# A two-layer decoder with experts: turned rows in the experts' order, gather rows split from the residual, router by slices

## The chip, the cores and the metric

The kernel runs on one core of a Trainium2 chip. The metric is the device time of one execution in microseconds (us), median of the runs. The core has PE (matrix engine, TensorE), DVE (vector), ACT (scalar), POOL and SP, each with its own instruction stream; they meet at semaphores. SP issues nearly all loads from HBM; sixteen DMA engines carry them. SBUF and PSUM (eight banks of 128 x 512 f32) are on chip.

## The reference

Batch 1, 256 tokens, width 1024, all f32, two layers. Cut to what matters here:

```python
h = rms_norm(x, norm2_g[l]) * (1.0 + sc2) + sh2        # sc2, sh2, g2: 1024 each, from c @ ada_w[l] + ada_b[l]
x = x + g2 * moe_ffn(h, ...)

scores = sigmoid(h @ w_router)                         # 64 experts in 8 groups
sel = scores + router_bias
gscore = sum of the two highest sel of each group; the 4 best groups are kept
idx = top 6 of sel among the kept groups
w = scores[idx] / sum(scores[idx]) * 2.5
routed = sum over chosen e of w_e * swiglu(h, w_gate_up[e], w_down[e])     # 1024 -> 2*256 -> 1024
shared = swiglu(h, shared_gate_up, shared_down)
```

Ahead of it stands an attention with norm and residual of its own in each layer (a dilated one in layer 0, a latent one in layer 1).

## The kernel before, in words

**Passes.** The experts of a layer are sorted by their count of tokens. `plan_passes` lays 64 experts in 22 passes of 128 slots (2 to 5 experts each). For each pass p PE gathers the tokens of its slots, with one-hot matrices `sel` that DVE makes out of `slot_of` or `slot_at` (`gather_half`, line 881: for two passes together, 256 slots, one half of the eight row groups at a time; 16 matmuls of `h_hi` and `h_lo` by `sel` per half). ACT copies the result into `xg` (`gathered`, 1335). `gate_up` (902) multiplies by the expert's weights in two halves, each of which frees its weight units; then silu, `hidden`, `middle` (transposes), `down` (944), and `scatter` (919) adds the rows back to tokens in banks 0 to 3, one pass late. The expert weights are stored with row p*8+k on partition p, so a gathered row group k holds rows p*8+k.

**Loads.** A unit is 1 MB of SBUF, 17 of them. The first experts (ranks 0 to 4) are fixed, as experts 0 to 4 are always placed first, and are loaded ahead (`EARLY_UNITS`, `LATE_UNITS`, `LAST_UNITS`). The others are chosen by count. SP waits for `order` (line 664), which says which expert has which rank, then issues each load as soon as its unit has been read by its user before (`wait_read`). The first, for pass 2, need half 0 and half 1 of passes 0 and 1 to be read; later ones need down projections.

**From the norm to pass 0.** `norm` on ACT (1282) and DVE (1529): sum of squares, square root, reciprocal, then two diagonal matrices `diag_r` with the tokens' scales. PE's `ada_sums` and `ada_columns` (729) turn a row of modulation (`row_of[g]`, copied from bank 7 by ACT in `ada_rows`, 1274) into columns with four matmuls; `norm_transposes` (713) multiplies x by `diag_r`, which turns and scales it at once: 16 matmuls of 128 contiguous columns of x into banks 0 to 3. DVE (banks 0, 2) and ACT (banks 1, 3) apply `amp` and `mod` and write hT, whose row group k holds rows k*128+p. In `experts` (845) PE computes the router's logits (16 matmuls, after all of hT), turns hT back into token rows (16 transposes), and a first half of the shared expert. ACT takes the sigmoid and copies the turned-back rows into `h_hi` as fp32r; `interleaved` (382) makes that write the rows in the order p*8+k. DVE does the routing (1604 on): biases, group maxima, a mask of groups by multiplying and adding, top six, `chosen`. It then computes `h_lo` = h - `h_hi`. PE forms ranks and counts; DVE makes `slot_of`, `sel`, `keys`, `hot`, `flag`; PE gathers pass 0 and 1, transposes the tables, and computes `order`, `places`, `at_ps`; `gate_up(0)` waits for `order`, then come `gate_up(1)` and the tables of overflow slots, which this input does not use.

An f32 matmul stands as two records in the trace, an fp32r one as one. Most matmuls pass through the helper on line 708, transposes through 711, ACT copies through 1234, SP loads of experts through 580 and of ring chunks through 548, so those lines stand for many places; the tile names tell them apart.

**In the attention of layer 0** SP's loads pass in one order: ring chunks of `kv_ada_w`, `w_router` (637), two rows of `router_bias` (640), two small ones, then ten chunks of `ada_w`, each as its ring place comes free. PE's `ada_columns(g)` for g=1, 2, 6, 4 stands between projections and heads.

## Time and profile before

| | |
|---|---|
| median of 3 runs | 1367.34 us (1365.87 to 1367.44) |
| the profiled execution | 1366.1 us, span of its instructions 1364.2 us, mean granted PE clock 0.933 |
| busy share | PE 82%, DVE 31%, ACT 19%, POOL 0% |
| moved from HBM | 500 MB, 367 GB/s over the span |

```profile
## 2 busy tenths in 40 slices
PE   6999887997798687777768889899779778777775
...
PEclk9998998999798899889889999899989979988979
DMA  9999996799999999999976715679999999999995
```

Each digit is a tenth of the busy share in one of 40 slices of 34 us. Slices 1 to 6 are the attention of layer 0, 7 to 20 its experts, 20 to 25 the attention of layer 1, the rest its experts. The DMA row is at 9 through the experts and lower about the beginning of each expert stage and in the attention of layer 1.

### The profile page before, as it was taken

The numbers are of one execution on the slowest core, as the hardware profiler recorded it, in microseconds if no ns is written. First come the engines' busy times: TensorE is split into PE (matmuls) and PEld (weight loads), VectorE is DVE, ScalarE is ACT, GpSimd is POOL, SyncE is SP. The second block draws the span as 40 slices with busy tenths as digits, with TensorE's granted clock in tenths as the row PEclk, the third lists the DMA queues.
The fourth block names the chain that finished last, engine by engine and source line by source line (L and its number), as shares of the span: only waits on it lengthen the run. The fifth ranks groups of instructions, "written<-read, shape, count | busy, mean of one in ns | idle before, by whom it ended". The sixth has DMA issues, their size and how long they took to land.

```text
span 1364.2 us, 17322 instructions
## 1 busy us (share of the span) xinstructions
PE 1114.0 (82%) x6720; PEld 619.4 (45%) x6720; DVE 422.6 (31%) x1026; ACT 253.1 (19%) x572; POOL 0.4 (0%) x5
## 2 busy tenths in 40 slices
PE   6999887997798687777768889899779778777775
PEld 4886466544243243233327467754424324322332
DVE  1397546321121121112132576532112112111213
ACT  1122513111011110101022263311101111010100
POOL 0000000000000000000000000000000000000000
PEclk9998998999798899889889999899989979988979
DMA  9999996799999999999976715679999999999995
GB/s 349 396 407 407 355 401 258 294 382 424 422 424 424 423 424 423 425 423 422 423 294 262 250 36 185 247 284 390 424 423 423 425 422 424 423 425 423 423 423 214
DMA packets 99914, 502.26 MB, mean 368 GB/s; under 512 B 11865, under 2 KB 37366, under 8 KB 44534
## 3 DMA queue, kind: packets, MB, share of 16 engines
q1 hardware_dynamic: 99366, 500.92, 90.1%
q8 instruction: 55, 0.90, 0.3%
q10 hardware_dynamic: 464, 0.20, 0.1%
q14 instruction: 29, 0.24, 0.0%
HBM read 500.04 MB, written 1.05 MB: 367 GB/s over the span
## 4 chain that ended last, share of the span: by engine, by line
SPq 42%; PE 33%; DMA 13%; DVE 6%; issue 4%; ACT 2%; DVEq 0%; ACTq 0%
SPq L580 39%; PE bank L708 27%; DMA w_gu<-in_moe_w_gate_up 4%; DMA w_gu_x<-in_moe_w_gate_up 4%; DMA ring<-in_ada_w 3%; SPq L666 3%; PE bank L1091 2%; DMA ring<-in_moe_w_gate_up 2%; PE bank L711 2%; PE bank L926 1%; DMA ring<-in_a_w_o 1%; DVE acc L1511 1%; PE bank L1072 1%; ACT p_sb L1311 1%; SPq L640 1%
## 5 line engine op out<-in xcount | busy, mean ns | idle before, releaser
L708 PE MATMUL bank<-w_gu,ring 128*32 128x512 f32 (+1 forms) x1088 | 341.5, 694 | 81.4 <-DMA w_gu<-in_moe_w_gate_up 55.5
L708 PEld LDWEIGHTS bank<-w_gu,ring 128*32 128x32 f32 (+1 forms) x1088 | 89.9, 134 | 213.1 <-issue 213.1
L708 PE MATMUL bank<-ring 128*32 128x512 f32 (+1 forms) x384 | 162.1, 689 | 21.6 <-DMA w_gu<-in_moe_w_gate_up 21.6
L708 PE MATMUL bank<-w_gu_x,ring 128*32 128x512 f32 (+1 forms) x320 | 144.6, 669 | 25.8 <-DMA w_gu<-in_moe_w_gate_up 21.2
L1729 DVE TENSOR_TENSOR hh<-sg,bank 128x256 f32<-128x256 f32 x44 | 27.4, 624 | 426.4 <-ACT sg L1344 426.4
L708 PE MATMUL bank<-w_gu,hhT 128*32 128x512 f32 (+1 forms) x576 | 147.2, 599 | 2.3 <-DMA w_gu<-in_moe_w_down 2.3
L708 PE MATMUL bank<-w_dn,ring 128*32 128x512 f32 x240 | 101.0, 788 | 24.0 <-DMA w_gu<-in_moe_w_gate_up 9.8
L1746 DVE SCALAR_TENSOR_TENSOR y_lo<-bank,w_slot,y_hi 128x512 fp32r<-128x512 f32 x88 | 62.0, 746 | 177.1 <-ACT y_hi L1234 177.1
L1344 ACT ACTIVATE sg<-bank 128x256 f32<-128x256 f32 x44 | 16.9, 384 | 504.7 <-PE bank L708 504.7
L708 PE MATMUL bank<-sel,h_hi 128*128 128x256 f32 x352 | 87.8, 289 | 0.0
L708 PE MATMUL bank<-sel,h_lo 128*128 128x256 f32 x352 | 84.2, 279 | 0.0
L1234 ACT ACTIVATE y_hi<-bank,w_slot 128x512 fp32r<-128x512 f32 x88 | 55.6, 683 | 149.4 <-PE bank L708 149.4
L926 PE MATMUL bank<-y_hi,st 128*128 128x512 f32 x176 | 73.7, 419 | 9.8 <-DVE y_lo L1746 9.8
L1234 ACT ACTIVATE ring<-bank 128x512 f32<-128x512 f32 x88 | 47.8, 595 | 156.1 <-PE bank L708 156.1
L1511 DVE SCALAR_TENSOR_TENSOR acc<-ring,csilu,acc 128x2048 f32<-128x2048 f32 x28 | 65.7, 2347 | 15.6 <-DMA ring<-in_ada_w 15.3
L926 PE MATMUL bank<-y_lo,st 128*128 128x512 f32 x176 | 69.2, 393 | 0.0
L708 PEld LDWEIGHTS bank<-w_gu_x,ring 128*32 128x32 f32 (+1 forms) x320 | 34.1, 130 | 75.1 <-issue 75.0
L708 PEld LDWEIGHTS bank<-sel,h_lo 128*128 128x128 f32 x352 | 66.5, 189 | 0.0
L708 PEld LDWEIGHTS bank<-sel,h_hi 128*128 128x128 f32 x352 | 66.0, 188 | 0.3
L708 PE MATMUL bank<-hT,ring 128*128 128x256 f32 (+2 forms) x192 | 61.3, 473 | 5.1 <-DMA w_gu<-in_moe_w_gate_up 5.1
L708 PEld LDWEIGHTS bank<-ring 128*32 128x32 f32 (+1 forms) x384 | 38.9, 133 | 58.2 <-issue 58.2
L708 PE MATMUL bank<-ring,hhT 128*32 128x512 f32 (+1 forms) x160 | 58.1, 596 | 0.6 <-DVE hhT L1736 0.6
(285 smaller groups left out, 1575.3 us busy)
## 6 DMA issues: line engine op xcount, KB each, us to landing
w_gu<-in_moe_w_gate_up SPq DMA_DIRECT2D x126, 1024.0 KB, 25.9
w_gu<-in_moe_w_down SPq DMA_DIRECT2D x68, 1024.0 KB, 26.3
ring<-in_ada_w SPq DMA_DIRECT2D x44, 1024.0 KB, 11.3
ring<-in_moe_w_gate_up SPq DMA_DIRECT2D x44, 1024.0 KB, 26.8
w_gu_x<-in_moe_w_gate_up SPq DMA_DIRECT2D x38, 1024.0 KB, 25.3
w_dn<-in_moe_w_gate_up SPq DMA_DIRECT2D x30, 1024.0 KB, 25.8
ring<-in_moe_w_down SPq DMA_DIRECT2D x16, 1024.0 KB, 26.1
w_dn<-in_moe_w_down SPq DMA_DIRECT2D x14, 1024.0 KB, 26.8
```

The source lines that it names most:

```text
L580: sp.dma_start(dst, src).then_inc(sem(f"unit_in{u}"), 16)
L640: sp.dma_start(bias_row[:, n, :], t["moe_router_bias"][n:n + 1, :].broadcast_to([P, E]))\
L666: index = {j: sp.value_load(tab_i[0:1, j:j + 1], min_val=0, max_val=E - 1) for j in sorted({j for _, j, _ in items if j != "shared"})}
L708: return nc.tensor.matmul(o, a, b, start=first, stop=last)
L711: return nc.tensor.transpose(o, a, const("ident")[0:rows, 0:rows])
L926: last = nc.tensor.matmul(bank[2 * ti + half][:, :], st[:, ti * P:(ti + 1) * P], y[:, half * 512:(half + 1) * 512], start=first and y is y_hi,
L1091: last = nc.tensor.matmul(bank[c][:, ti * N:(ti + 1) * N], hT[:, 2 * j + k, ti * P:(ti + 1) * P], qkv_rows[j][:, k, c * N:(c + 1) * N], st ...
L1234: return nc.scalar.activation(o, i, ACT.Copy, **kw)
L1344: nc.scalar.activation(sg[:, :], bank[b][:, 0:FE], ACT.Silu).then_inc(sem(f"silu_done{l}"), 1)
L1511: ins = v.scalar_tensor_tensor(out=acc[:, :], in0=w, scalar=csilu[:, k:k + 1], in1=acc[:, :], op0=ALU.mult, op1=ALU.add)
L1729: v.tensor_tensor(hh[:, :].rearrange("s (f p) -> s p f", f=FE // P), sg[:, :].rearrange("s (p f) -> s p f", f=FE // P), bank[b][:, FE:2 * ...
L1746: last = v.scalar_tensor_tensor(out=y_lo[:, c], in0=bank[6 + half][:, :], scalar=w_slot[:, :], in1=y_hi[:, c].bitcast(F32), op0=ALU.mult, ...
```

## The change

**Row order.** `norm_transposes` takes every eighth column of x (`every_8th`) in norms 1 and 3, so hT's group k holds rows p*8+k. `w_router`, the shared gate and up weights, the shift, the scale and the norm gain are brought into that order: by other access patterns of the loads, by `ada_columns`, which for those rows takes every eighth element of a strip with 16 matmuls of 64 weights instead of four of 128, and by a small tile `rows_pk`, filled by three loads on ACT's queue near the start.
**Gather rows.** `h_hi` and `h_lo` are split from the raw x times the token's scale, in norm (ACT copies x to `h_hi`, DVE subtracts), both written contiguously. The gathers read every eighth column of them. The shift and scale are applied afterwards, when ACT moves the gathered rows (`gathered`: four Identity operations with bias and scale instead of two copies). The 16 transposes back and the four strided copies and subtractions fall away.
**Order of work.** The router's matmuls follow slice by slice behind hT. A dummy sigmoid brings ACT's table load into norm. `row_of` is copied by DVE. The shared half is split in pieces around ranks, gather and places. `order` and `places` come before the tables; `gate_up(0)` no longer waits for `order`; the table transposes and `at_ps` go between the halves of passes 0 and 1; in layer 1 the gate's two matmuls go from the norm to between passes 0 and 1. DVE's group mask is one operation instead of five.

```diff
-            h_hi = sb("h_hi", [P, NT, KT, P], F32R, scope=moe)
+            h_hi = sb("h_hi", [P, NT, D], F32R, scope=moe)
+        def every_8th(tokens, k):
+            return tokens[:, k:k + D - KT + 1:KT]
...
-                                 t["moe_w_router"].rearrange("l (k p) e -> p (l k) e", p=P)).then_inc(sem("router_in"), 16)
+                                 t["moe_w_router"].rearrange("l (p k) e -> p l (k e)", p=P)).then_inc(sem("router_in"), 16)
...
+                            tokens = x[:, ti, k * P:(k + 1) * P] if n == 2 else every_8th(x[:, ti, :], k)
-                if n == 3:
-                    gate_half(3, 0)
-                    gate_half(3, 1, 6)
...
+                strips = {3: 4, 6: 4, 4: 2}.get(g, 0)
+                for m in range(4 if strips else 0):
+                    last = mm(bank[7][:, m:4 * strips:4], row_of[g][:, m * P:(m + 1) * P], const("quarters")[:, 0:strips], True, True)
+                if strips < 4:
+                    q0, at = (2, 2 * strips + 4 * (strips > 0)) if g in (1, 4) else (0, 0)
+                    for u in range(2):
+                        for k in range(KT):
+                            last = mm(bank[7][64 * u:64 * u + 64, at + k:at + k + 1], every_8th_of_strip(row_of[g], k),
+                                      const("quarters")[:, q0 + u:q0 + u + 1], True, True)
...
-                for j in range(4):
-                    ti, half = j // 2, j % 2
-                    for k in range(4):
-                        last = tr(bank[j][:, k * P:(k + 1) * P], hT[:, 4 * half + k, ti * P:(ti + 1) * P])
-                    last.then_inc(sem("h_ps"), 1)
-                                last = mm(o, h[:, ti, 4 * half + kk, :], sel[:, ti, :], ti == 0 and h is h_hi,
+                                last = mm(o, every_8th(h[:, ti, :], 4 * half + kk), sel[:, ti, :], ti == 0 and h is h_hi,
-                    if p == 0:
-                        pe.wait_ge(sem("order"), l + 1)
+                gate_up(0)
...
+                if l == 1:
+                    for half, b in enumerate((3, 7)):
+                        mm(bank[b][:, :], const("quarters")[:, 2 + half:3 + half].broadcast_to([P, P]), row_of[5][:, :], True, True)\
+                            .then_inc(sem("gate_ps"), 1)
+                gate_up(1, (0,))
...
-                gate_up(0)
-                gate_up(1)
+                gate_up(1, (1,))
...
+            for n in range(2):
+                act.dma_start(rows_pk[:, n, 0:2, :], t["ada_b"][n:n + 1, 3 * D:5 * D].rearrange("a (s p k) -> p (a s) k", p=P, k=KT))\
+                   .then_inc(sem("mask_in"), 16)
+            act.dma_start(rows_pk[:, :, 2, :], t["norm2_g"].rearrange("l (p k) -> p l k", k=KT)).then_inc(sem("mask_in"), 16)
-                    ada_rows(ADA_IN_WO[n // 2])
+                    nc.scalar.activation(small[:, 34:35], eps_c, ACT.Sigmoid)
+                    act.wait_ge(sem("xn_ready"), 2 * n + 2)
+                    copy(h_hi[:, 0, :], x[:, 0, :], scale=small[:, 4:5]).then_inc(sem("h_act"), 1)
-                        last = copy(xg[l][i % 2][:, k:k + 2, :].rearrange("p k c -> p (k c)"), bank[banks[b]][:, :])
+                        last = nc.scalar.activation(xg[l][i % 2][:, k, :], bank[banks[kk // 2]][:, (kk % 2) * N:(kk % 2 + 1) * N],
+                                                    ACT.Identity, bias=mod[:, 24 + 48 * l + k:25 + 48 * l + k], scale=amp[:, 1 + 2 * l, k:k + 1])
...
+                        last = v.scalar_tensor_tensor(out=h_lo[:, ti, :], in0=x[:, ti, :], scalar=small[:, 4 + ti:5 + ti],
+                                                      in1=h_hi[:, ti, :].bitcast(F32), op0=ALU.mult, op1=ALU.subtract)
-                link(V, v.tensor_tensor(gmask[:, :, :], gleft[:, :, 0:G], gsc[:, :, 0:G], ALU.not_equal))
...
+                link(V, v.tensor_tensor(gmask[:, :, :], gleft[:, :, 0:G], gsc[:, :, 0:G], ALU.is_equal))
+                link(V, v.scalar_tensor_tensor(out=ch, in0=gmask[:, :, :].unsqueeze(3).broadcast_to([P, NT, G, 8]), scalar=-big, in1=ch,
+                                               op0=ALU.mult, op1=ALU.add))
-                for j in range(4):
-                    dve.wait_ge(sem("h_act"), 4 * l + j + 1)
-                    v.tensor_tensor(interleaved(h_lo, j), in_order(bank[j]), interleaved(h_hi, j).bitcast(F32), ALU.subtract)\
-                        .then_inc(sem("h_dve"), 1)
```

## Rows read from the trace of the kernel before

**Rows 1.** page, part 3: the DMA queue of ACT's loads: packets, MB, share of 16 engines
```profile
q10 hardware_dynamic: 464, 0.20, 0.1%
```

**Rows 2.** windows: length, busy PE, PEld, DVE, ACT, POOL; PE clock, DMA share, GB/s
```profile
144.00:152.00 8.00, 6.33 (x66) 3.23 (x64) 6.36 (x29) 6.24 (x23) 0.00 (x0) 1.00 0.54 136
...
230.00:252.00 22.00, 20.30 (x128) 14.63 (x128) 15.92 (x68) 6.35 (x9) 0.00 (x0) 1.00 0.22 72
270.00:280.00 10.00, 9.87 (x64) 5.54 (x68) 2.17 (x5) 2.36 (x4) 0.00 (x0) 1.00 0.74 291
...
863.00:869.00 6.00, 5.70 (x26) 5.70 (x27) 1.82 (x6) 0.36 (x2) 0.00 (x0) 0.50 0.97 388
1000.00:1300.00 300.00, 234.04 (x1408) 102.05 (x1408) 53.49 (x112) 36.80 (x67) 0.00 (x0) 0.91 1.01 424
```

**Rows 3.** timeline of the SP queue in the attention of layer 0 (start, length)
```profile
139.24 7.64 SPq L640 DMA_DIRECT2D bias_row<-in_moe_router_bias  x2
...
147.87 19.45 SPq L548 DMA_DIRECT2D ring<-in_ada_w  x10
```

**Rows 4.** timeline of the SP queue, layer 0, first loads of the chosen experts
```profile
249.93 1.43 SPq L580 DMA_DIRECT2D w_gu_x<-in_moe_w_gate_up  x2
...
278.30 0.33 SPq L580 DMA_DIRECT2D xn<-in_moe_w_gate_up  x1
```

**Rows 5.** timeline, layer 0, from the norm to the first pass (start us, length us)
```profile
216.07 1.87 PE L708 MATMUL bank<-cst,kT 128*128 128x4 f32 x8 [2.26 <-ACT kT L1234]
...
217.80 5.37 PE L708 MATMUL bank<-xn,x 128*128 128x128 f32 x32
...
224.33 3.75 PE L708 MATMUL bank<-w_router,hT 128*128 128x64 f32 x32 [1.16 <-issue]
...
232.35 0.48 DVE L1628 TENSOR_TENSOR choice<-choice,gleft 128x64 f32<-128x64 f32 x2
...
234.51 3.85 DVE L1638 TENSOR_TENSOR h_lo<-bank,h_hi 128x512 fp32r<-128x512 f32 x4
...
235.69 0.31 PEld L708 LDWEIGHTS bank<-cst,chosen 128*64 128x64 f32 x4
...
239.69 0.28 PE L708 MATMUL bank<-sel,h_lo 128*128 128x256 f32 x1
...
243.23 0.28 PE L708 MATMUL bank<-sel,h_lo 128*128 128x256 f32 x1
...
245.04 1.10 PE L708 MATMUL bank<-hot,rtT 64*128 64x64 f32 x8 [0.35 <-DVE rtT L1709]
...
246.07 3.65 PE L708 MATMUL bank<-w_gu_x,ring 128*64 128x512 f32 x16
```

**Rows 6.** timeline, layer 1, the same place
```profile
863.30 1.87 PE L708 MATMUL bank<-cst,kT 128*128 128x4 f32 x8 [2.56 <-ACT kT L1234]
...
870.86 1.88 PE L708 MATMUL bank<-kT,cst 128*128 128x512 f32 x4
```

**Rows 7.** groups by line and form: weight loads, DVE (| busy us, mean ns)
```profile
L708 PEld LDWEIGHTS bank<-sel,h_lo 128*128 128x128 f32 x352 | 66.5, 189 | 0.0
...
L1638 DVE TENSOR_TENSOR h_lo<-bank,h_hi 128x512 fp32r<-128x512 f32 x8 | 7.7, 1030 | 0.0
...
L1600 DVE TENSOR_TENSOR x<-x,junk 128x512 f32<-128x512 f32 x8 | 5.5, 692 | 0.3
...
L1614 DVE TENSOR_TENSOR gsc<-gsort 128x16 f32<-128x16 f32 x2 | 0.4, 187 | 0.1
...
L1621 DVE TENSOR_TENSOR gmask<-gleft,gsc 128x16 f32<-128x16 f32 x2 | 0.3, 174 | 0.1
```

**Rows 8.** timeline behind pass 0 (ACT, PE), and a group of ACT by form
```profile
263.90 1.09 ACT L1234 ACTIVATE ring<-bank 128x512 f32<-128x512 f32 x2 [3.38 <-PE bank L708]
...
264.01 3.65 PE L708 MATMUL bank<-w_dn,hhT 128*64 128x512 f32 x16
...
L1292 ACT ACTIVATE hT<-bank,mod,amp 128x256 f32<-128x256 f32 x12 | 6.1, 559 | 17.8 <-PE bank L708 17.8
```

More of the change, by code:

```diff
@@ L845, in experts, with shared_part @@
             def experts(l):
+                n = 2 * l + 1
                 pe.wait_ge(sem("router_in"), 16 * 5)
[L848 to L860 removed]
+                for j, (ready, turn) in enumerate((("hT_dve", 2 * n + 3), ("hT_act", 2 * n - 1), ("hT_dve", 2 * n + 4),
+                                                   ("hT_act", 2 * n))):
+                    pe.wait_ge(sem(ready), turn)
+                    for k in (2 * j, 2 * j + 1):
+                        for ti in range(NT):
+                            last = nc.tensor.matmul(bank[4][:, ti * E:(ti + 1) * E], hT[:, k, ti * P:(ti + 1) * P],
+                                                    w_router[:, l, k, :], start=k == 0 and ti == 0, stop=k == KT - 1,
+                                                    skip_group_check=True)
+                last.then_inc(sem("logits"), 1)
+                def shared_part(j, f, b, k0, k1):
                     w = use(("sgu", l, j))
[L862 removed]
+                    for k in range(k0, k1):
                         last = mm(bank[b][:, f * N:(f + 1) * N], w[:, k, f * P:(f + 1) * P], hT[:, k, :], k == 0, k == KT - 1)
[L864 removed]
+                    if f == FE // P - 1 and k1 == KT:
                         used(("sgu", l, j), last)
[L867 to L868 removed]
+                pe.wait_ge(sem("gate_sb"), 4 * l + 2)
+                shared_part(0, 0, 6, 0, KT)
+                shared_part(0, 1, 6, 0, 4)
                 pe.wait_ge(sem("chosen"), l + 1)
@@ L898, in gather_pair, with gate_up @@
                             for h in (h_hi, h_lo):
-                                last = mm(o, h[:, ti, k, :], sel[:, ti, 0:P], ti == 0 and h is h_hi, ti == NT - 1 and h is h_lo)
+                                last = mm(o, every_8th(h[:, ti, :], k), sel[:, ti, 0:P], ti == 0 and h is h_hi, ti == NT - 1 and h is h_lo)
                     last.then_inc(sem(f"gath_done{l}"), 1)
-                def gate_up(p):
+                def gate_up(p, halves=(0, 1)):
                     pe.wait_ge(sem(f"xg_ready{l}"), 2 * (p // 2) + 2)
-                    if p == 0:
-                        pe.wait_ge(sem("order"), l + 1)
-                    elif p >= 2:
+                    if p >= 2:
                         pe.wait_ge(sem(f"st_ready{l}"), p)
-                    for half in range(2):
+                    for half in halves:
                         for j in positions(p):
@@ L1294, in norm @@
                     last.then_inc(sem("hT_act"), 1)
+                    if n != 2 and j == 1:
+                        copy(h_hi[:, 1, :], x[:, 1, :], scale=small[:, 5:6]).then_inc(sem("h_act"), 1)
             def attention(l):
@@ L1330, in experts @@
                     .then_inc(sem("score"), 1)
-                for j in range(4):
-                    act.wait_ge(sem("h_ps"), 4 * l + j + 1)
-                    copy(interleaved(h_hi, j), in_order(bank[j])).then_inc(sem("h_act"), 1)
                 def gathered(i, half, banks=(4, 7)):
                     act.wait_ge(sem(f"gath_done{l}"), 2 * i + half + 1)
-                    for b in (1, 0):
-                        k = 4 * half + 2 * b
-                        last = copy(xg[l][i % 2][:, k:k + 2, :].rearrange("p k c -> p (k c)"), bank[banks[b]][:, :])
+                    for kk in range(4):
+                        k = 4 * half + kk
+                        last = nc.scalar.activation(xg[l][i % 2][:, k, :], bank[banks[kk // 2]][:, (kk % 2) * N:(kk % 2 + 1) * N],
+                                                    ACT.Identity, bias=mod[:, 24 + 48 * l + k:25 + 48 * l + k], scale=amp[:, 1 + 2 * l, k:k + 1])
                     last.then_inc(sem(f"xg_ready{l}"), 1)
@@ L1371, in experts @@
                         act.wait_ge(sem(f"gath_done{l}"), p + 1)
-                        for b, k in ((7, 4), (4, 0)):
-                            last = copy(xg[l][0][:, k:k + 4, 0:P], bank[b][:, :].rearrange("p (k c) -> p k c", c=P))
+                        for k in range(KT):
+                            last = nc.scalar.activation(xg[l][0][:, k, 0:P], bank[4 if k < 4 else 7][:, (k % 4) * P:(k % 4 + 1) * P],
+                                                        ACT.Identity, bias=mod[:, 24 + 48 * l + k:25 + 48 * l + k],
+                                                        scale=amp[:, 1 + 2 * l, k:k + 1])
                         last.then_inc(sem(f"xg_ready{l}"), 1)
@@ L1529, in norm @@
             def norm(n, outs):
+                if n != 2:
+                    g = ADA_IN_WO[n // 2]
+                    dve.wait_ge(sem("ada_sums"), SUMS_TURN[g])
+                    v.tensor_copy(row_of[g][:, :], bank[7][:, :]).then_inc(sem("row_sb"), 1)
                 norm_scale(n)
```

108 lines of the change are left out of this document (53 added, 55 removed).

## The prediction

> **What bounds the kernel now.** I read the windows first, then the SP timeline, then PE, ACT and DVE between the norm and the first expert pass. In the passes the DMA engines are full: 424 GB/s at a share of 1.01 over 300 us, while PE is busy 234 of them [rows 2]. There a faster or slower engine is worth nothing as long as the load queue stays full. The time can only move where that queue runs dry. It does so at three kinds of place. (1) In the attention of layer 0 it moves 136 GB/s for 8 us [rows 2], behind SP's load of the router and its bias [rows 3]. (2) Before the first pass of each layer all prefetched units are full; the queue stands at 72 GB/s from 230 to 252 us [rows 2] until half 0 of pass 0 has been read, and the first chosen expert is requested at 249.93 [rows 4]. (3) It is dry once more, 0.74 in 270 to 280 [rows 2], until pass 1's down projection is over and units come free at 278.30 [rows 4]. From there it is full to the end of the layer. So the gain of a layer is not how much earlier pass 0 begins, but how much earlier pass 1 ends, since ten loads of 1 MB are through by then in both cases.
>
> **The path before pass 0, layer 0, step by step.** All of it is PE, ACT and DVE in series [rows 5].
> Row copy: `row_sb` moves from ACT, where it stood behind the square root, to DVE right behind `ada_sums`. The 128x512 copy costs about 0.69 like other DVE work of that size [rows 7]; DVE is idle there. PE's columns begin at 214.85 instead of 216.07: 1.2 off. Layer 0's columns (g=3) keep their 8 records.
> Router: it now follows each slice of hT instead of all of it. Its last quarter of 3.75 us [rows 5] is 0.95. The transposes (5.4 us, [rows 5]) end near 222.0; ACT turns the last slice until 223.3, though its copy to h_hi and a table load are now ahead of it (the load falls into its idle time, and the copy ends at 222.3). Logits at 224.35 instead of 228.1: 3.7 off, the 1.2 included.
> Routing chain on DVE: two multiplies, two adds, one scale and two memsets give way to one operation. The adds alone took 0.48 [rows 5], the multiplies as much; the saving is 1.15. Chosen at about 229.8 for 234.6: 4.8 off.
> Split: h_lo's 3.85 us stood between `chosen` and `slot_of` [rows 5]; it goes into DVE's waits in the norm, where two operations of 1024 columns at about 1.2 us fit beside the transposes. The 16 turns of hT on PE go as well. PE now needs 1.4 us for the ranks, DVE about 1.1 for slots and selection: the gather starts at 232.3 instead of 239.5, 7.2 off.
> After the gather: 2.8 us lay before pass 0. Now there are the order and places (0.9), a quarter of the shared half (0.9), and the wait for ACT, whose evacuation is four Identity operations of 0.56 (about 1.95 in a row) instead of two copies in 1.09 [rows 8]: 2.2. **Pass 0 starts 7.8 us earlier**, near 238.25 [rows 5]. The order is ready at 236.5, well before SP can use it.
> What is moved behind it: the table transposes (0.65) and `at_ps` (1.10, [rows 5]) now stand between the halves of passes 0 and 1. They were ahead of pass 0, so they count against the 7.8 at the place that matters, the end of pass 1: +1.7. DVE's copies of the tables and its selection for the next pass end some 2 us before PE is through with the second half of pass 1; half the cover would be left if each took 1 us more.
> ACT's longer evacuation, once per pass: it starts at 263.90 and would end at 265.85; the down projection (264.01, 3.65 long, [rows 8]) needs the bank for its second half at 265.85. That is a tie, 0.1 per pass, 0.2 in all.
> Layer 0: 7.8 - 1.7 - 0.2 = **5.9 us off**.
>
> **Layer 1.** The same, with two differences. Its columns (g=5) are now 32 narrow records instead of 8 in 1.87 us [rows 6]. Four weight loads of 64 columns took 0.31 at full clock [rows 5], some 0.06 apart; at the half clock granted here [rows 2] twice that, so 3.7 for 1.87, which costs 1.85 and eats the early start. The two gate matmuls (four records, 1.88, [rows 6]) leave the norm, where PE would otherwise have waited for hT for most of that time, so 0.4 is gained, and they come back between passes 0 and 1 for 1.75. 5.9 - 1.85 + 0.4 - 1.75 = **2.7 off**.
>
> **Ahead of that.** The router's weights are read in rows of 2 KB instead of 256 bytes: 256 pieces for 2048. SP's bias load behind it took 7.64 us for two small loads [rows 3]; the next ada chunks went out only at 147.87. The DMA engines lost 8 x (1 - 136/424) = 5.4 us. From there to the first pass the chain is DMA, so that is returned almost whole, unless the hold is backlog of other loads. Bounds 0 and 5.4. Against it stand the columns of g=1, 2 and 4: 72 more narrow records, 4 us of PE in the attention, 2 of them before SP's router load; I take **4.5 off**.
> The three new ACT loads fetch 768 pieces of 32 bytes. The ACT queue's 464 packets took 0.1% of 16 x 1364 us, 47 ns each [rows 1], so 48 pieces per engine cost up to 2.3 us beside the first weight block, for which PE waits. Bounds 0 and 2.3; I take **+1.5**, nearer to the upper end since that block is what the start waits for.
>
> **The term that nothing in the trace shows: strided weight loads.** hT's transposes, every gather and the narrow columns now load PE's weights with a step of 32 bytes. Before, all were contiguous. A load of 128 columns takes 189 ns [rows 7] and gathers follow each other in 117 ns, from 239.69 to 243.23 for 31 [rows 5], so the weight load (107 of it for the columns) is what sets the gather's pace as much as the 256 columns do. A lower bound is 0. The upper bound comes from DVE: with a strided output 512 columns took 1030 ns, without 692 [rows 7], 0.66 ns more per element, up to about 1.7 ns each; reading every 8th element cost 187 for 174 with 16 elements, 0.8 ns each [rows 7]. At 1.7 ns the 128 columns take 107 ns longer. Transposes: 24 full-clock records, +2.6. First gather: 32, +3.4. Both gathers before the end of pass 1: +3.4. That is 9.4 per layer, 1.7 more for layer 1's columns, and 1.5 in the attention: 22 us. I take 0 as the likelier end, because PE has its own read path, of which these DVE rows show nothing, and PE's moving operand shows it fetching twice as fast as its weights are; but the opposing rows are the nearest there are, and the price is as large as the gain.
> The Trainium skill speaks against the change here: SBUF — State Buffer, section "Door 1: The DMA port swizzle", says that SBUF is fetched in lines of 16 bytes and that accesses which leave the line every time pay. A step of 32 bytes does. DVE's rows agree with it; no row here shows it for PE. By that rule the time is that of the first rival; without it, that of the sum.
>
> **Sum.** -5.9 - 2.7 - 4.5 + 1.5 = -11.6, on the profiled execution's 1366.1: 1354.5. The median of the runs stands 1.2 above it, so 1355.8.
>
> **Rivals.**
> *Strided weight loads at half pace* (slower). 1355.8 + 22 = 1377. It decides from a price of about 55 ns per load on, where the gain is gone. For it: DVE's two rows. Against: in the passes PE has 66 of 300 us free [rows 2], so the other 18 gathers of each layer cost nothing. 31%.
> *The early pass is given back*: pass 0 moves, pass 1 does not, since the tables between the halves make DVE's selection late, or the SP hold is backlog and stays. Without the router's 4.5 and half of the layers' 8.6 the time is 1364.5. For it: the hold begins while earlier loads are still landing. 15%.
> *The clock stays up*: before the columns in both layers PE is idle 2.3 to 2.6 us and then runs at 0.50 (863 to 869, [rows 2]). The idle time becomes 1.1 to 1.3. If it does not fall, up to 3 us a layer come back: 1351. It is a part of the likeliest case's range.
> *The change does not do what it says*, as more passes or other experts: the routing is the same arithmetic; 1%.
>
> **How the numbers follow.** Forecast 53%: 1350 to 1361. Given back 15%, 1361 to 1369. Strided 31%, 1369 to 1378. To leave out no more than two in ten the range must reach into the strided case: 1349 to 1378. A measurement of this kernel can tell about 0.2%, 2.7 us, from no change. Faster: 53, two thirds of 15, and a light price of the stride: 64%. Same: 9%. Slower: 27%.
>
> **What would show it.** Gathers 117 ns apart, or 220. Weight loads of h_lo 189 ns, or near 300. Pass 0 at 238 less what was gained ahead. SP's two bias loads in 1 to 2 us, not 7.6. In 144 to 152 us above 400 GB/s. The interval from the last attention matmul to the first chosen load shorter by 7 to 8 us, and that to the end of pass 1 by 6. I am wrong if the gathers keep their pace and the time still does not fall, or if the window before pass 0 shortens and the end of the layer stays.

## The result, and the profile after

| | kernel before | changed kernel |
|---|---|---|
| median | 1367.07 us (4 runs) | 1396.36 us (4 runs, 1387.44 to 1397.49) |
| ratio | | 1.0212, 95% interval 1.0166 to 1.0257 |
| profiled execution | 1366.1 us | 1387.4 us, span 1385.6, mean granted PE clock 0.947 |
| PE busy | 82% | 86% |

The change costs 29 us (a fifth execution, not in the median, took 1401.33) where I had forecast a gain of 12. The profiled execution of the changed kernel is its fastest one; it is 21 above that of before. So 8 of the 29 us aren't in the trace.

The groups by line and form say first what is different (busy us, mean ns of one):

```profile
L709 PEld LDWEIGHTS bank<-sel,h_lo 128*128 128x128 f32 x352 | 118.9, 338 | 0.0
...
L1353 ACT ACTIVATE ring<-bank,mod,amp 128x256 f32<-128x256 f32 x176 | 84.9, 563 | 256.5 <-PE bank L709 256.5
...
L1577 DVE SCALAR_TENSOR_TENSOR h_lo<-x,small,h_hi 128x1024 fp32r<-128x1024 f32 x4 | 5.1, 1275 | 0.0
...
L709 PEld LDWEIGHTS bank<-cst,kT 128*64 128x64 f32 x32 | 3.5, 216 | 2.1 <-DVE kT L1559 2.1
```

A weight load of 128 columns of `h_lo` takes 338 ns for 189 [rows 7], one of 64 narrow columns 216. The operations that I had sized from other rows came out as sized: ACT's evacuation 563 ns (559 in [rows 8]), DVE's h_lo 1275 for my 1.2 us. The timeline of layer 0, PE unless marked, shows what that does to the pace. It answers to [rows 5]:

```profile
95.10 3.55 PE L709 MATMUL bank<-cst,ada_row 128*64 128x1 f32 x32
...
191.76 4.43 PE L709 MATMUL bank<-cst,ada_row 128*128 128x2 f32 x40
...
218.72 1.04 PE L709 MATMUL bank<-acc,cst 128*1 128x512 f32 x8
220.98 1.05 PE L709 MATMUL bank<-cst,kT 128*128 128x4 f32 x8 [1.21 <-DVE kT L1559]
222.55 7.91 PE L709 MATMUL bank<-xn,x 128*128 128x128 f32 x32 [0.52 <-DVE xn L1550]
230.29 3.68 PE L860 MATMUL bank<-w_router,hT 128*128 128x64 f32 x32
...
239.43 1.26 PE L709 MATMUL bank<-chosen,cst 128*128 128x64 f32 x10 [0.21 <-DVE chosen L1668]
...
241.90 0.41 PE L709 MATMUL bank<-sel,h_lo 128*128 128x256 f32 x1
...
249.13 0.40 PE L709 MATMUL bank<-sel,h_lo 128*128 128x256 f32 x1
...
251.55 3.65 PE L709 MATMUL bank<-w_gu_x,ring 128*64 128x512 f32 x16 [0.21 <-ACT ring L1353]
```

Thirty gathers lie between 241.90 and 249.13: 241 ns apart, for 118 in [rows 5]. The transposes take 7.91 us for 5.37. Pass 0 begins at 251.55, 5.5 us later than before; I had said 7.8 earlier, and more with what was to be gained ahead. `ada_sums`, where my path begins, is at 218.72 for 212.76: 6.0 us are lost ahead of it already. The SP queue shows the two other places (start, length), which answer to [rows 3] and [rows 4]:

```profile
143.97 1.21 SPq L641 DMA_DIRECT2D bias_row<-in_moe_router_bias  x2
...
146.25 22.56 SPq L549 DMA_DIRECT2D ring<-in_ada_w  x10
...
255.41 0.89 SPq L581 DMA_DIRECT2D w_gu_x<-in_moe_w_gate_up  x2
...
289.79 0.33 SPq L581 DMA_DIRECT2D xn<-in_moe_w_gate_up  x1
```

The end of pass 1, my measure of a layer, moves from 278.30 to 289.79. And the windows (columns as in [rows 2]):

```profile
144.00:152.00 8.00, 8.00 (x84) 3.93 (x82) 6.38 (x29) 5.75 (x22) 0.00 (x0) 1.00 0.80 313
230.00:252.00 22.00, 21.58 (x124) 19.45 (x126) 10.83 (x69) 5.64 (x12) 0.00 (x0) 1.00 0.32 135
...
280.00:290.00 10.00, 10.00 (x48) 6.41 (x50) 1.18 (x3) 2.21 (x5) 0.00 (x0) 1.00 0.39 162
1000.00:1300.00 300.00, 252.76 (x1404) 124.41 (x1396) 53.91 (x114) 49.16 (x97) 0.00 (x0) 0.94 1.01 421
```

In 230 to 252 the queue moves 135 GB/s for 72, since the last prefetched units are asked for later than before; the dry place ahead of pass 1's end is now 280 to 290, at a share of 0.39. The last row holds a thing I had not looked for. In the passes PE has 47 of 300 us free, so it isn't the bound, the DMA share is 1.01 as before, and still 421 GB/s are moved and not 424. Over some 850 us of passes that is 6 us.

### The profile page after: what moved, and what is told of

Read it like the earlier page. It is cut to its first block, busy times and chain, and to the rows that moved or that the text cites. A ratio compares the mean times of both kernels' runs of the same rounds, so it can differ in the third digit from the quotient of the medians.

```text
span 1385.6 us, 17545 instructions
## 1 busy us (share of the span) xinstructions
PE 1186.8 (86%) x6792; PEld 702.0 (51%) x6792; DVE 419.7 (30%) x1017; ACT 286.1 (21%) x656; POOL 0.4 (0%) x5
## 3 DMA queue, kind: packets, MB, share of 16 engines
HBM read 500.07 MB, written 1.05 MB: 362 GB/s over the span
## 4 chain that ended last, share of the span: by engine, by line
PE 42%; SPq 36%; DMA 13%; DVE 4%; issue 4%; ACT 2%; DVEq 0%; ACTq 0%
PE bank L709 34%; SPq L581 33%; DMA w_gu<-in_moe_w_gate_up 4%; DMA w_gu_x<-in_moe_w_gate_up 4%; SPq L667 2%; PE bank L1101 2%; DMA ring<-in_moe_w_gate_up 2%; PE bank L930 2%; DMA ring<-in_ada_w 2%; PE bank L712 2%; PE bank L967 1%; DMA ring<-in_a_w_o 1%; ACT p_sb L1329 1%; PE bank L1082 1%; PE bank L860 1%
## 5 line engine op out<-in xcount | busy, mean ns | idle before, releaser
L709 PE MATMUL bank<-w_gu,ring 128*32 128x512 f32 (+1 forms) x1088 | 315.5, 651 | 73.3 <-DMA w_gu<-in_moe_w_gate_up 51.4
L709 PE MATMUL bank<-w_gu,hhT 128*32 128x512 f32 (+1 forms) x576 | 154.5, 607 | 0.0
L709 PE MATMUL bank<-sel,h_hi 128*128 128x256 f32 x352 | 146.3, 416 | 0.0
L709 PE MATMUL bank<-sel,h_lo 128*128 128x256 f32 x352 | 141.7, 403 | 0.0
L1353 ACT ACTIVATE ring<-bank,mod,amp 128x256 f32<-128x256 f32 x176 | 84.9, 563 | 256.5 <-PE bank L709 256.5
L709 PE MATMUL bank<-w_gu_x,ring 128*32 128x512 f32 (+1 forms) x320 | 126.5, 607 | 8.8 <-DMA w_gu<-in_moe_w_gate_up 5.7
L709 PEld LDWEIGHTS bank<-sel,h_lo 128*128 128x128 f32 x352 | 118.9, 338 | 0.0
L709 PEld LDWEIGHTS bank<-sel,h_hi 128*128 128x128 f32 x352 | 118.2, 336 | 0.1
L709 PE MATMUL bank<-w_dn,ring 128*32 128x512 f32 x240 | 83.1, 678 | 12.7 <-DMA w_gu_x<-in_moe_w_gate_up 9.2
L1771 DVE TENSOR_REDUCE w_slot<-bank 128x1 f32<-128x256 f32 x44 | 18.7, 424 | 145.2 <-PE bank L712 145.2
## 6 DMA issues: line engine op xcount, KB each, us to landing
w_gu<-in_moe_w_down SPq DMA_DIRECT2D x68, 1024.0 KB, 26.5
```

The costliest lines, as they stand in the source:

```text
L709: return nc.tensor.matmul(o, a, b, start=first, stop=last)
L1353: last = nc.scalar.activation(xg[l][i % 2][:, k, :], bank[banks[kk // 2]][:, (kk % 2) * N:(kk % 2 + 1) * N], ACT.Identity, bias=mod[:, 24 ...
L1771: v.tensor_reduce(w_slot[:, :], bank[5][:, 0:N], AX_X, ALU.add)
```

## The experiments

All of them are timed beside the kernel before on the same chip (its medians there: 1367.0 to 1368.3). Places are given as in the prediction: ada_sums, pass 0, end of pass 1.

### The strided weight loads

**a_gather, a_all, b_stride, deint.** The stride taken out of the changed kernel's gathers, then of all its weight loads, put into the gathers of the kernel before, and (deint) moved from PE to ACT and DVE.

```diff
 # a_gather (a_all does the same for norm_transposes and ada_columns)
-last = mm(o, every_8th(h[:, ti, :], 4 * half + kk), sel[:, ti, :], ...
+last = mm(o, h[:, ti, (4 * half + kk) * P:(4 * half + kk + 1) * P], sel[:, ti, :], ...
 # b_stride: the kernel before
-last = mm(o, h[:, ti, 4 * half + kk, :], sel[:, ti, :], ...
+last = mm(o, every_8th(h[:, ti, :, :], 4 * half + kk), sel[:, ti, :], ...
 # deint: h_hi, h_lo are [P, NT, KT, P]; by_k(row) = row.rearrange("t (q k) -> t k q", k=KT)
-copy(h_hi[:, 0, :], x[:, 0, :], scale=small[:, 4:5])
+copy(h_hi[:, 0, :, :], by_k(x[:, 0, :]), scale=small[:, 4:5])
```

> The changed kernel with one thing undone: the gathers load 128 contiguous columns of h_hi and h_lo, not every 8th (the experts then get other columns of the residual, so what they compute is changed). Theory 1, the strided weight load is what was lost: gathers 117 ns apart again instead of 242, the first gather 3.9 us shorter, the two before the end of pass 1 4.0 shorter, the same in layer 1: 15.8 us off the changed kernel, 1371.6 against its profiled 1387.4 and 1380 against its median of 1396. Theory 2, the loss is the narrow columns, the clock and the moved order: gathers get faster, the time stays above 1385.

> The changed kernel with all three strided weight loads made contiguous: gathers, transposes of the norms, and the narrow column matmuls (the values in them are then other ones). Theory 1: 15.8 us off for the gathers, 2.6 per layer for the transposes, and 96 narrow loads at 137 instead of 216 ns, 7.6 in all of which some 6 lie on a path that PE sets: 27 off, 1360 profiled and 1369 by the median. If the stride were all that my forecast missed, it would come to 1356. Theory 2: no lower than 1375.

> The kernel before with the gathers alone reading every 8th column of h_hi and h_lo (other columns than the experts want, so what they compute is changed). Theory 1: gathers 242 ns apart, 3.9 us in the first gather of each layer and 4.0 in the two before the end of pass 1: 1367 + 15.8 = 1383. Theory 2: gathers are longer but the passes hide all but the first, 1371 to 1375.

> The changed kernel, but ACT and DVE read the raw residual with the stride while they write h_hi and h_lo in expert order, so that the gathers load contiguous columns; what is computed stays the same. Theory 1: as much off as without the stride in the gathers, 15.8 us, if the copies of 1.13 (ACT) and 1.27 us (DVE) grow by no more than a factor of 2, since PE's transposes take 7.9 us beside them: 1371.6 profiled, 1380 by the median. Rival: the strided read on ACT or DVE takes so long that the last slices of hT come late, and each us of it comes back twice, once per layer: 1385.

| | median us | ratio to before | ada_sums L0 | pass 0 L0 | end of pass 1 L0 |
|---|---|---|---|---|---|
| before | 1368.3 | | 212.76 | 246.07 | 278.30 |
| changed | 1396.4 | 1.0212 | 218.72 | 251.55 | 289.79 |
| a_gather | 1419.4 | 1.0380 | 219.72 | 248.67 | 286.24 |
| a_all | 1373.6 | 1.0034 | 218.36 | 244.87 | 280.74 |
| b_stride | 1421.5 | 1.0391 | 214.48 | 251.29 | 289.03 |
| deint | 1387.6 | 1.0151 | 219.18 | 248.14 | 285.70 |

The times of a_gather and b_stride say nothing on the stride. Other values come out of layer 0, layer 1 then chooses other experts, and one more pass is run: 368 gathers of each kind for 352, 508.6 MB moved for 502.3. I hadn't thought of that when I chose an edit that changes the data. Their layer 0 up to the end of pass 1, which comes ahead of it, can be read: from ada_sums to pass 0 it takes 28.95 us without the stride in the gathers and 32.83 with it (3.9 less), and b_stride 36.81 for the 33.31 of before.

a_all computes other values too, but has the same number of passes and moves the same 502.3 MB as the changed kernel. It is 23 us faster; I had expected 27. deint, which computes the same, gains 9 where 16 were expected. Its gathers are back at 189 ns a load, and these are the copies that now carry the stride:

```profile
L1247 ACT ACTIVATE h_hi<-x,small 128x1024 fp32r<-128x1024 f32 x4 | 8.6, 2140 | 0.0
L1580 DVE SCALAR_TENSOR_TENSOR h_lo<-x,small,h_hi 128x1024 fp32r<-128x1024 f32 x4 | 8.3, 2078 | 0.6 <-ACT h_hi L1247 0.6
```

The strided read takes ACT 2140 ns for 1138 and DVE 2078 for 1275, but it stays beside PE's transposes: the first gather of layer 0 follows ada_sums after 22.85 us, as in the changed kernel (22.86). So it isn't this rival that eats the 7 us. Up to pass 0 deint gains what was expected, 3.9 us in each layer. From pass 0 to the end of pass 1 it gains 0.7 in layer 0 (37.56 for 38.24) and 2.0 in layer 1 (39.29 for 41.32), where 4.0 were expected. There the granted clock falls where that of the changed kernel's trace stays up. In two windows of deint, then in the same two of the changed kernel:

```profile
262.00:266.00 4.00, 4.00 (x12) 1.10 (x10) 1.43 (x8) 0.00 (x0) 0.00 (x0) 0.57 1.01 426
274.00:280.00 6.00, 4.17 (x15) 3.41 (x16) 1.70 (x3) 0.74 (x2) 0.00 (x0) 0.72 0.99 389
```

```profile
262.00:266.00 4.00, 4.00 (x30) 2.73 (x28) 2.08 (x8) 0.00 (x0) 0.00 (x0) 1.00 1.01 426
274.00:280.00 6.00, 3.54 (x16) 1.12 (x13) 1.50 (x3) 2.31 (x5) 0.00 (x0) 1.00 0.82 294
```

One such fall costs 1.7 us, by the block of b_order below. Two in layer 0 and one more than the changed kernel's in layer 1 (0.72 in 920 to 926, for 1.00) are 5.1, so 15.8 become 10.7; in the traces it is 10.5. Why they fall in one kernel and not in the other isn't shown.

**b_nat** puts a price on the strided gathers alone, on unchanged data: it writes the rows in plain order and reads them with the step.

```diff
 # the kernel before, h_hi and h_lo [P, NT, D]
 def interleaved(h, j):
-    return h[:, j // 2, :, :].rearrange("t k (c q) -> t c q k", c=KT)[:, 4 * (j % 2):4 * (j % 2) + 4, :, :]
+    return h[:, j // 2, 512 * (j % 2):512 * (j % 2) + 512]
 # gathers: h[:, ti, k, :]  ->  h[:, ti, k:k + D - KT + 1:KT]
```

> The kernel before with h_hi and h_lo written in natural order (a contiguous write for ACT and DVE instead of one with a step) and the gathers reading every 8th column; it computes the same. The stride theory: gathers 242 ns apart, first gather 3.9 us longer, the two before the end of pass 1 4.0 longer together, DVE's h_lo 1.4 shorter: 6.5 per layer, 1380. If the passes hid the later gathers: 1372.

1388.6 us, ratio 1.0166 (1.0144 to 1.0189): 20.8 us for the gathers of both layers, more than the 12.5 expected. The weight load and the gathers' pace are those of the changed kernel, and the writes of h_lo got shorter (ACT's of h_hi too, 602 ns for 1088):

```profile
L711 PEld LDWEIGHTS bank<-sel,h_lo 128*128 128x128 f32 x352 | 119.2, 339 | 0.0
...
L1641 DVE TENSOR_TENSOR h_lo<-bank,h_hi 128x512 fp32r<-128x512 f32 x8 | 5.0, 681 | 0.0
```

The first gather is 3.9 longer, as expected. From pass 0 to the end of pass 1 it takes 37.8 us for 32.2 in layer 0 and 37.7 for 32.2 in layer 1, 5.5 where two gathers of 16 loads at 123 ns make 4.0. The rest is about one fall of the clock, which in layer 0 stands at 0.66 in 275 to 280. DVE's 1.4 gave nothing: from `chosen` to the first gather it is 4.74 for 4.84. From the end of pass 1 to that of the passes of layer 0 (the next layer's first load of `b_w_dq`) it takes 426.5 us for 426.0: the other gathers are indeed hidden behind the DMA, as the prediction had it.

### The alignment of the weight buffers

In the compiled kernel before, `ring` begins at byte 33920 of a partition, 128 past a multiple of 256, and so do `w_gu_x`, `w_gu_0`, `w_dn`, `xn` and `hT`: 13 of the 17 units lie in these. `w_gu_1`, 4 units, begins at 195840, a multiple of 256. The change adds `rows_pk`, 192 bytes, ahead of it; it lies at 195520 then, 192 past. (The changed kernel also takes 512 bytes of DMA scratch for 1024, which my list of the change doesn't name, so all its tiles begin 512 bytes lower. That moves no distance to a multiple of 256; it was not tried alone.)

```diff
 # b_shift: the kernel before
 amp = sb("amp", [P, 5, KT])
+pad = sb("pad", [P, 48])
 # b_align: 32 instead of 48, and pad_x = sb("pad_x", [P, 32]) ahead of x
 # a_pad: the changed kernel
 rows_pk = sb("rows_pk", [P, 2, 3, KT])
+pad = sb("pad", [P, 16])
```

> The kernel before with one unused tile of 192 bytes per partition put where the changed kernel has rows_pk. It computes the same. In the passes the changed kernel moves 421 GB/s, and so do its variants with contiguous gathers, while the kernel before moves 424; with gathers made strided it still moved 424. Theory A: the 192 bytes shift the buffers w_gu_1 (4 of the 17 units) off the boundary on which they lay, and each 8 KB piece written there takes longer: 421 GB/s here too, 3 us per layer, 1373. Theory B: the rate is lost to ACT's longer evacuation or another engine's traffic: 424 GB/s, 1367 to 1368.

> The kernel before with two unused tiles of 128 bytes per partition, so that ring, w_gu_x, w_gu_0 and w_dn (128 bytes past a multiple of 256 before) and w_gu_1 (on a multiple before) all begin at a multiple of 256 bytes. Theory A, if what counts is the distance to a multiple of 256: the other 13 units get faster too, 426 to 430 GB/s in the passes and 1352 to 1362. If only 64-byte steps below 128 count, or under theory B: 424 GB/s and 1367.

> The changed kernel with 64 unused bytes per partition behind rows_pk, so that w_gu_1 lies on a multiple of 256 bytes again, as before the change. It computes the same. Alignment theory: 424 GB/s in the passes instead of 421 and 5.7 us off, 1390 by the median. Rival, the rate of the changed kernel is lost to ACT's longer evacuation as well: less than 2 us off.

| | w_gu_1 past 256 | the 13 others | GB/s, 1000 to 1300 | median us | ratio |
|---|---|---|---|---|---|
| before | 0 | 128 | 424 | 1367.8 (a_pad's: 1367.0) | |
| b_shift | 192 | 128 | 421 | 1373.5 | 1.0050 (1.0032 to 1.0068) |
| b_align | 0 | 0 | 427 | 1358.5 | 0.9938 (0.9917 to 0.9959) |
| a_pad | 0 | 128 | 423 | 1390.3 | 1.0171 (1.0152 to 1.0190) |

Windows of 1000 to 1300, b_shift, then b_align:

```profile
1000.00:1300.00 300.00, 239.07 (x1409) 104.56 (x1407) 54.65 (x115) 37.90 (x69) 0.00 (x0) 0.89 1.01 421
```

```profile
1000.00:1300.00 300.00, 235.94 (x1444) 106.06 (x1448) 53.44 (x113) 37.02 (x68) 0.00 (x0) 0.92 1.01 427
```

An unused tile alone makes the kernel before 5.7 us slower, and aligned buffers make it 9 faster. 64 unused bytes make the changed one 6.0 faster by the medians. That fits, but its interval and the changed kernel's (1.0166 to 1.0257) overlap, so by itself it would not show it. That the rate is lost to ACT's evacuation falls: a_pad has it and runs at 423.

### What is left without stride and shift

**a_all_pad** is a_all with the 64 bytes; it too computes other values in the same number of passes.

> The changed kernel with contiguous weight loads in gathers, transposes and columns (the values in them are then other ones) and with w_gu_1 on a multiple of 256 bytes again. If only the stride and the alignment were missing in my forecast, it gives 1356. If the narrow columns (4.8 by the added ones), the tables moved between the halves and terms I over-valued before the gather also count, 1367 to 1369, the same as before.

1359.1 us, ratio 0.9950 (0.9932 to 0.9968). The stride in all three places is the 31.2 us between a_pad and this. The forecast was 1355.8, so it is 3 us off once both are out. The expectation that other terms would bring it back to 1367 was wrong. But the parts of the sum do not hold, as the next runs show.

**b_cols** adds narrow columns to the kernel before, on unchanged data, with the step of the change.

```diff
 # ada_columns of the kernel before
+for m in range({1: 12, 2: 12, 4: 16, 5: 12}.get(g, 0)):
+    u, k = m % 2, m // 2
+    last = mm(bank[7][64 * u:64 * u + 64, 16 + k:17 + k], row_of[g][:, k:k + 512 - KT + 1:KT],
+              const("quarters")[:, u:u + 1], True, True)
```

> The kernel before with 12 narrow strided matmuls added to the columns of g=1, 2 and 5 and 16 to those of g=4, their results unused, so that each issues 32 records (g=4: 40) as in the changed kernel; it computes the same. Theory: PE sets the path from 20 to 120 us and again from 181 us to the norm, so g=1 and g=4 add 2.6 and 3.5 us in full, g=2 1.8 of which the DMA-bound ring loads return most, g=5 some 2 to 4: ada_sums of layer 0 5 to 6 us later, 1373 to 1376. Rival: what comes before 180 us is returned in the DMA-bound stretch and only 3.5 is left in layer 0, and the ada_sums wait of 2.6 us on DVE swallows most of that: 1368 to 1370.

1372.6 us, ratio 1.0045 (1.0025 to 1.0064): 4.8, at the lower edge of the expectation. In its trace, one of the slower of its executions (1376.98), `ada_sums` of layer 0 comes 9.5 us later, not the 5 to 6 expected. And it doesn't price the change's columns in full: it has as many records, but only 24 of 32 are narrow ones, and they alternate between the two halves of the output, where the change does one half and then the other. They take 2.49 us for 3.55. Without the stride those of the change would cost less; the same 32 records in a_all_pad take 1.82 us. In b_cols, then in a_all_pad:

```profile
97.71 2.49 PE L708 MATMUL bank<-cst,ada_row 128*128 128x4 f32 x32
```

```profile
97.70 1.82 PE L710 MATMUL bank<-cst,ada_row 128*64 128x1 f32 x32
```

**b_early, b_order, b_best, b_order_al.** Three parts of what the change does before the gather (not the split into the norm), without stride or new columns; the order ahead of the tables on top (b_order); and each of the two with aligned buffers (b_best, b_order_al).

```diff
 # b_early: the kernel before, with the change's hunks for
 #  norm on DVE: v.tensor_copy(row_of[g][:, :], bank[7][:, :]), no ada_rows in ACT's norm
 #  the router's loop over four slices of hT, each behind its own wait
 #  gmask by is_equal and one scalar_tensor_tensor; the memsets ahead of the wait for score
 # b_order: b_early, and on PE behind gather_half(0, 1, ...)
-tables; flags -> order, places; at_ps; gate_up(0); gate_up(1); tables of overflow
+flags -> order, places; gate_up(0); tables; gate_up(1, (0,)); at_ps; tables of overflow; gate_up(1, (1,))
```

> The kernel before with the three parts of the change that need no stride and no new columns: the row copy on DVE, the router slice by slice, the shorter mask arithmetic on DVE. It computes the same. By the changed kernel's rows: 1.1 for the row copy, 1.2 for the router's wait (its 3.7 us of PE work cannot start before the transposes end), 1.1 for the mask: chosen and pass 0 3.4 us earlier per layer, 1361. If my forecast's sizes held: router 2.5 and mask 1.15, 4.85 per layer, 1358. Rival, the early pass is given back: 1366 or more.

> The kernel before with those three parts and with all weight buffers on multiples of 256 bytes. It computes the same. Both add up: 9 us for the alignment and 6.8 for the parts, 1352. If what the parts gain is swallowed because the loads are now faster or slower to follow: 1358.

> b_early with the order and places computed right behind the gather and the table transposes and at_ps moved between the halves of passes 0 and 1. It computes the same. Theory: pass 0 begins 2.1 us earlier (0.65 for the transposes, 1.10 for at_ps, 0.35 of waiting), and all but the 0.35 comes back before the end of pass 1: between pass 0 and that end 34.0 us instead of 32.2, 1360 to 1361 beside 1361.0 for b_early. If the interruptions of PE in pass 0 and 1 also let the granted clock fall, 1362 to 1365. Rival: the earlier first half of pass 0 lets SP ask for the first chosen experts earlier and that is a gain: 1357.

> b_order with all weight buffers on multiples of 256 bytes. It computes the same. Theory: 8.5 less than b_order, as b_best stands to b_early: 1352. Rival as above: 1349.

| | median us | ratio to before | pass 0 L0 | end of pass 1 L0 | pass 0 L1 | end of pass 1 L1 |
|---|---|---|---|---|---|---|
| before | 1367.0 | | 246.07 | 278.30 | 894.26 | 926.49 |
| b_early | 1361.0 | 0.9957 (0.9942 to 0.9973) | 244.21 | 276.44 | 889.09 | 921.32 |
| b_order | 1366.6 | 0.9985 (0.9975 to 0.9994) | 242.86 | 280.08 | 891.22 | 928.47 |
| a_all_pad | 1359.1 | 0.9950 | 240.82 | 276.71 | 882.58 | 921.90 |
| b_best | 1352.5 | 0.9888 (0.9870 to 0.9906) | 242.16 | 274.39 | 885.37 | 919.16 |
| b_order_al | 1356.9 | 0.9922 (0.9900 to 0.9944) | 239.51 | 275.05 | 883.10 | 920.36 |

The ratios of b_order and b_order_al are to the kernel before beside them, 1368.1. b_early comes to the expected 1361 and b_best to the expected 1352. b_order and b_order_al miss theirs, 1360 to 1365 and 1352. b_order begins pass 0 1.35 us earlier and ends pass 1 3.6 later: 37.2 us between the two for 32.2, in both layers. What was moved there (0.65 and 1.10) is 1.8 of it. The rest can be seen in its timeline of PE, and in windows, of b_early and then of b_order:

```profile
250.43 3.65 PE L708 MATMUL bank<-w_gu,ring 128*64 128x512 f32 x16
254.02 1.10 PE L708 MATMUL bank<-hot,rtT 64*128 64x64 f32 x8
...
256.51 5.35 PE L708 MATMUL bank<-w_gu,ring 128*64 128x512 f32 x16
```

```profile
250.00:260.00 10.00, 10.00 (x57) 4.25 (x52) 0.81 (x3) 0.77 (x2) 0.00 (x0) 1.00 0.98 397
270.00:280.00 10.00, 10.00 (x74) 4.60 (x76) 3.99 (x10) 2.36 (x4) 0.00 (x0) 1.00 0.74 283
```

```profile
250.00:260.00 10.00, 10.00 (x52) 4.74 (x53) 3.59 (x13) 0.37 (x1) 0.00 (x0) 0.86 1.01 427
258.00:260.00 2.00, 2.00 (x6) 0.48 (x4) 0.14 (x2) 0.00 (x0) 0.00 (x0) 0.50 1.03 434
270.00:280.00 10.00, 9.64 (x48) 6.20 (x52) 1.39 (x4) 1.09 (x2) 0.00 (x0) 0.83 0.50 197
```

The last half of gate_up, split off behind a stretch of small matmuls, takes 5.35 us for 3.65, as the clock is at 0.50 for a part of it, and the clock falls again in 270 to 280. In b_early both windows are at 1.00. The same 5.35 stands at 904.87 in layer 1 of b_order and at 897.95 in layer 1 of a_all_pad. Two falls of 1.7 us are 3.4 of the 5.0 us, the moved work the rest. So this part costs 7.3 us between the two traces (3.6 and 3.7 from `ada_sums` to the end of pass 1), 5.5 by the medians and 3.8 by the ratios, which set each beside its own kernel before.

That the small matmuls bring the falls is likely, but not proved. From pass 0 to the end of pass 1 the kernels with the old order and contiguous gathers (before, b_early, b_cols, b_shift, b_align, b_best) take 32.2 us in eleven of twelve layers, without a fall, and b_best's layer 1 has one (33.8, 0.83 in 910 to 920). b_order has two in each layer, b_order_al one and two. But the changed kernel's own trace has the new order and none there in layer 0, and b_nat has the old order and one in each layer.

b_best beats both kernels: 1.1% below the one before and 44 us below the changed one.

## Why the prediction was wrong

**The step that failed** is "I take 0 as the likelier end", for the strided weight loads. I had the upper bound, the rows of DVE, and a rival at 1377 with 31%. The argument against it was that PE has its own read path. That path pays for the step too: a load of 128 columns at a step of 32 bytes took 149 ns more, 123 in the pace of the gathers, above the upper bound of 107. b_nat, which gives the kernel before this step in its gathers and nothing else but shorter writes, is 20.8 us slower. DVE's 1.7 ns per strided element was the nearest row and close. The rule that speaks against the change, in the Trainium skill, SBUF — State Buffer, section "Door 1: The DMA port swizzle" (lines of 16 bytes, an access that leaves the line pays), agrees with what the weight loads show at this step; other steps were not tried. The decision "the other 18 gathers cost nothing" was right (b_nat, 426.5 for 426.0).

**The rival's size** was short too: 22 us for a measured 31.2. By b_nat 20.8 of it is gathers, where I had 13.6. The transposes are 2.4 in layer 0 (7.91 against 5.47 in a_all_pad) for my 2.6. In layer 1 they are 1.4 by a_all_pad (7.92 against 6.54) and 4.1 by a_all (3.84): the contiguous ones get shorter with the clock, while the strided ones take 7.9 wherever its fall lies. Four groups of columns at up to 1.7 (3.55 for 1.82) make up the rest. The transposes were not tried alone. What I didn't count is that the granted clock falls at other places than before; in the passes 0 and 1 such falls come on top.

**The step that wasn't there** is the alignment: 6 us (b_shift 5.7). The prediction costs each instruction of the change but not the tile it adds.

Then, by its own steps. For the first, the windows of before, then of the changed kernel:

```profile
216.00:224.00 8.00, 7.10 (x40) 6.91 (x40) 2.58 (x8) 1.82 (x5) 0.00 (x0) 0.68 0.99 412
```

```profile
216.00:224.00 8.00, 6.27 (x35) 4.63 (x35) 3.10 (x10) 3.39 (x8) 0.00 (x0) 1.00 0.86 288
222.00:230.00 8.00, 7.48 (x32) 7.45 (x32) 4.33 (x10) 4.38 (x6) 0.00 (x0) 0.79 0.98 399
```

- Row copy: 1.2 forecast; the columns follow ada_sums after 2.26 us for 3.31, 1.05. Right. They also take 1.05 for 1.87, since the clock stood at 1.00 and not 0.68 in 216 to 224. But it fell right behind them, beneath the transposes (0.79 in 222 to 230). So "the clock stays up" did not come true; the fall moved. Nor was the shorter idle time the reason: b_cols still waits 2.55 us there, and its columns take 1.05 too.
- Router: wrong by an error in my sum. I let the last quarter (0.95) follow the last slice of hT, though PE's 3.7 us of router work can't start before its own transposes end. Only the wait of 1.16 [rows 5] goes. 3.7 was forecast, the copy included; without the stride it is 1.16 + 1.05. With the steps below, a_all_pad comes from `ada_sums` to pass 0 in 26.5 us for 33.3: 6.8 earlier for my 7.8.
- Mask: 1.15 forecast; from the router's start to the ranks it is 9.14 for 10.32, 1.18. Right.
- Split into the norm: a gain of 2.4 forecast from `chosen` to the gather; it is 2.15 us for 4.84, 2.7. Right.
- After the gather 2.2 us forecast: it is 2.42. Right. ACT's evacuation, a tie: the down projection takes 3.81 for 3.65. Right.
- Tables between the halves: +1.7 forecast, with no gain of its own; b_order puts the whole part at 4 to 7 us for both layers. The term had the work and not the clock. It is the rival "the early pass is given back" by another mechanism than I gave it: DVE's selection wasn't late (PE's longest wait in 245 to 290 is 2.5 us for `y_lo`, in before, b_early, b_order and the changed kernel alike).
- Layer 1's columns: 3.7 forecast for 32 records at half clock; 3.55 measured with the stride, in the changed kernel with the clock down for the last part, in a_pad at 1.00 throughout. The right number for the wrong reason.
- Ahead: 4.5 off forecast; `ada_sums` comes 6.0 later. SP's hold went as I said, 1.21 us for 7.64, but 313 GB/s stand in 144 to 152 for 136, not above 400. From the router's load to the Wo matmuls, with the columns behind both, it takes 39.7 us (143.35, 183.09) in the changed kernel, 41.9 in a_all_pad and 42.7 before (138.75, 181.41). b_cols has the hold, asks for the router as late (144.31), and takes 42.6 (186.90). So of the 6.7 us of hold 0.8 to 3.4 came back in the five traces that have the router's new rows (deint 39.3): the larger part was backlog, as one rival had it. Against it, PE has nothing free from 20 to 120 us in the trace of before (100.00 busy of 100) and carries the added columns: the router's load is asked for 4.6 us later in the changed kernel (143.35 for 138.75). And behind the Wo matmuls the columns of g=4 take 4.43 for 0.95, 3.5 more. I had 4 us for all of them. The three small loads of ACT: 1.5 forecast; the first ada matmul starts at 13.21 for 12.51, 0.7, but in b_order, without them, at 13.31, so no price is shown.

Per layer, in the kernel that has neither stride nor shift, from ada_sums to the end of pass 1: 62.4 for 65.5 us in layer 0, 3.1 gained for a forecast of 5.9; 67.6 for 66.8 in layer 1, 0.8 lost for a forecast gain of 2.7. That its median is nearly the forecast one is thus in part luck: in that trace 3.8 us are gained between the end of layer 0's passes and the next loads (50.2 us for 54.0), a place where the change does nothing but where the trace of the changed kernel shows the same 50.2 and others, a_all, b_order and b_early, 54.0. I can't say what makes it so.

**What stays open.** Why the changed kernel's executions spread over 10 us (14 with the fifth), and a_all's over 19 (1361.9 to 1380.6), where those of the kernel before spread over 5 to 7. The mean granted clock goes with it: in a_all it is 0.934 in the fastest and 0.921 in the slowest, in the changed kernel 0.947 in the fastest, the one with the trace, and 0.939 to 0.943 in the others. That fits falls at places that differ from one execution to the next, but one trace per kernel doesn't show it. And what decides where the clock falls.

## What to carry to other kernels

A strided read doesn't vanish when it moves to another engine: find out how often each engine reads the data, and give the step to the one that reads each element once (b_nat's writers gain 0.35 us per 512 columns on DVE and 0.49 on ACT, its 704 weight loads lose 0.15 us each). Before a tile is added ahead of DMA targets, look where those end up modulo 256 bytes, and align them all: here that was worth 9 us for no instruction at all. Small matmuls put into a dense stretch of PE cost more than their length if the granted clock falls behind them, as in b_order, so an earlier start bought with them has to be measured at the place that frees the loads.

## What the hardware showed that I had not expected

**DMA targets.** With 8 KB pieces per partition and all 16 DMA engines busy, the passes move 421 GB/s when 4 of 17 buffers begin 192 bytes past a multiple of 256 and the rest 128 past, 424 when those 4 are on a multiple, 427 when all are. The Trainium skill, DMA: Bandwidth & Descriptors, section "How a descriptor splits into AXI transactions", says that a descriptor is cut at multiples of 256 bytes and that one which starts between them needs more beats; by its arithmetic, as an estimate, a piece of 8 KB needs 4 to 6 beats more than 256, 1.6 to 2.3%. The page tells it of reads. Here only the target in SBUF was moved, so it shows at the write, of the same order but not in the same proportion: by the size of buffers (an estimate, if all units carry equal loads) 0.9% at 128 past and 3.0% at 192 past.

**Weight loads.** 128 columns at a step of 32 bytes: 338 ns for 189, gathers 241 ns apart for 118. 64 columns: 216 ns, and 32 records of them in 3.55 us for 1.82; in 2.49 with the step where they alternate between the halves of the output (b_cols).

**The granted clock** fell to its lower level, 1.2 GHz, behind short, small matmuls in the middle of a stretch in which PE was busy all the time (0.50 in 258 to 260 of b_order, 0.86 in 250 to 260, PE busy 10.00 of 10). I had only looked for it behind idle time.
